# A peer step's second slab as moving operand of 512 columns, with results kept by tokens

## What is computed

```
def rmsnorm(x, g):                       # per token, over 1024 features
    y = x * rsqrt(mean(x * x) + 1e-6)
    return y * g
x = x + merged @ w_out                   # end of the first mixer
# peer_ffn(h): every token uses some of 16384 experts with weights gate
act = gelu(expert_u[idx] . h)
x = x + sum(gate * act * expert_v[idx])
x = rmsnorm(x, norm_final_g)             # end of the first block
# second block, layer 0
x = x + 0.5 * swiglu(rmsnorm(x, norm_ffn1), w_gate, w_up, w_down)
```

## Time and profile before

| | us |
|---|---|
| median of 3 runs | 2274.48 (2274.35 to 2275.05) |
| time of the profiled execution | 2271.26 |
| its span, first to last instruction | 2269.5 |
| TensorE busy in it | 2091.3 (92%) |
| VectorE busy | 1536.9 (68%) |
| ScalarE busy | 1036.3 (46%) |
| GpSimd busy | 67.7 (3%) |
| mean granted clock of TensorE | 0.97 |

### The profile page before, as it was taken

How to read it: one execution, slowest core, us unless ns; L and a number is a source line. 1 busy time by engine, 2 the same in 40 slices (tenths; PEclk the granted TensorE clock), 3 DMA queues, 4 the chain that set the end, 5 groups by cost and what they waited for, 6 DMA issues and landing times.

```text
span 2269.5 us, 45414 instructions
## 1 busy us (share of the span) xinstructions
PE 2091.3 (92%) x16952; PEld 2052.1 (90%) x16952; DVE 1536.9 (68%) x2526; ACT 1036.3 (46%) x1467; POOL 67.7 (3%) x41
## 2 busy tenths in 40 slices
PE   7898962789999999999999999979999999999997
PEld 7898862679999999999999999869999999889997
DVE  5677699976666666666667655676557555856555
ACT  4444320334444444444445554545445444555443
POOL 0000240000000000000000100000000000000000
PEclk9999985999999999999999999999999999999999
DMA  5334420015555555555554555425555555444553
GB/s 192 114 129 157 142 101 0 0 44 179 182 180 183 185 185 179 182 181 181 183 185 162 170 181 187 138 88 172 186 175 167 191 177 186 131 131 158 185 180 107
DMA packets 95684, 348.19 MB, mean 153 GB/s; under 512 B 10752, under 2 KB 10880, under 8 KB 95360
## 3 DMA queue, kind: packets, MB, share of 16 engines
q1 hardware_dynamic: 95184, 344.88, 46.2%
q10 hardware_dynamic: 432, 2.36, 0.3%
HBM read 346.15 MB, written 1.05 MB: 153 GB/s over the span
## 4 chain that ended last, share of the span: by engine, by line
PE 79%; DVE 14%; issue 3%; ACT 3%; DVEq 0%; DMA 0%; SPq 0%; ACTq 0%
PE front L1555 37%; PE acc L1555 29%; PE tile L1555 12%; DVE w_lo L901 2%; DVE pick L1333 2%; ACT w_hi L571 1%; DVE pick L1338 1%; DVE h_lo L933 1%; DVE rstd L925 1%; DVE onehot L1312 0%; DVE onehot L1316 0%; DVE idx L1320 0%; DVE top_i L1258 0%; DVE rest L1251 0%; DVE top_i L1247 0%
## 5 line engine op out<-in xcount | busy, mean ns | idle before, releaser
L901 DVE TENSOR_TENSOR w_lo<-raw,w_hi 128x1024 fp32r<-128x1024 f32 x636 | 783.5, 1232 | 204.1 <-ACT w_hi L571 203.6
L571 ACT CAST w_hi<-raw 128x1024 fp32r<-128x1024 f32 x652 | 679.5, 1043 | 372.4 <-PE front L1555 137.3
L1555 PE MATMUL front<-h_hi,w_hi 128*128 128x256 f32 x2432 | 690.2, 284 | 6.0 <-DVE h_lo L933 4.9
L1555 PE MATMUL front<-h_lo,w_hi 128*128 128x256 f32 x2432 | 688.2, 283 | 0.0
L1555 PE MATMUL front<-h_hi,w_lo 128*128 128x256 f32 x2432 | 688.1, 283 | 0.0
L1555 PE MATMUL acc<-mid_hi,w_hi 128*128 128x256 f32 x1728 | 491.4, 284 | 12.4 <-DVE mid_lo L1002 12.4
L1555 PE MATMUL acc<-mid_hi,w_lo 128*128 128x256 f32 x1728 | 490.4, 284 | 0.0
L1555 PE MATMUL acc<-mid_lo,w_hi 128*128 128x256 f32 x1728 | 490.3, 284 | 0.0
L1555 PEld LDWEIGHTS front<-h_hi,w_hi 128*128 128x128 f32 x2432 | 466.7, 192 | 8.0 <-DVE h_lo L933 5.6
L1555 PEld LDWEIGHTS front<-h_lo,w_hi 128*128 128x128 f32 x2432 | 466.8, 192 | 0.1
L1555 PEld LDWEIGHTS front<-h_hi,w_lo 128*128 128x128 f32 x2432 | 466.8, 192 | 0.0
(11 more groups left out here) (247 smaller groups left out, 1968.9 us busy)
## 6 DMA issues: line engine op xcount, KB each, us to landing
raw<-stream SPq DMA_DIRECT2D x652, 512.0 KB, 3.3
x<-x_t SPq DMA_DIRECT2D x2, 512.0 KB, 4.6
keysT<-keys_t ACTq DMA_DIRECT2D x1, 1024.0 KB, 6.5
attc<-attention_constants ACTq DMA_DIRECT2D x1, 1024.0 KB, 4.8
out_t<-h SPq DMA_DIRECT2D x4, 256.0 KB, 2.2
mixc<-mixer_constants SPq DMA_DIRECT2D x1, 704.0 KB, 9.0
wpool<-w_pool ACTq DMA_DIRECT2D x1, 256.0 KB, 5.1
lane<-lanes SPq DMA_DIRECT2D x1, 128.0 KB, 4.7
```

The source lines that it names most:

```text
L571: nc.scalar.copy(w_hi[:, s, :], raw[:, s, :]).then_inc(hi_ready, 1)
L901: nc.vector.tensor_tensor(w_lo[:, s, :], raw[:, s, :], w_hi[:, s, :].bitcast(F32), ALU.subtract).then_inc(lo_ready, 1)
L1555: return nc.tensor.matmul(out, lhsT, rhs, start=start, stop=stop, **kw)
```

## The change

In the peer steps the operands of `drain` change places. `mid` becomes stationary (128 experts x 128 tokens, one half of the tokens at a time) and the slab moves, 512 features at once: four banks (two token halves x two feature halves) with three matmuls each, 12 of 512 columns in the place of 24 of 256. `acc` then holds tokens on the partitions. The seeding follows: 16 matmuls of 128 columns with `x` as stationary operand in the place of 8 of 256.

At the end (`turn_x`) the sum of squares of a token is one row sum: ScalarE squares two banks with `accum_out`, takes the root of 128 x 1, VectorE inverts it and scales the banks into `x_tokens` (one quarter by ScalarE), TensorE turns 16 tiles of 128 x 128 back to features (identity kept in `eye`), and VectorE and ScalarE in turn, pair by pair, write `x` with the gain. `x` is then final, and the MLP behind starts with the ordinary norm. `weighted_norm`, `square_weights`, `gain_product`, `rstd_x`, the second root and GpSimd's four scalings of `x` are gone.

```diff
                     begin = s == 0 and not seeded and turn is None
-                    for m in range(KT):
+                    for b in range(4 if seeded else 0):
+
+                        a, c = [part[:, s % 2, b // 2 * P:(b // 2 + 1) * P] for part in (mid_hi, mid_lo)]
+                        hi, lo = [part[:, n % RING, b % 2 * D // 2:(b % 2 + 1) * D // 2] for part in (w_hi, w_lo)]
+                        mm(banks[:, b, :], a, hi, False, False, skip_group_check=True)
+                        mm(banks[:, b, :], c, hi, False, False, skip_group_check=True)
+                        ins = mm(banks[:, b, :], a, lo, False, False, skip_group_check=True)
+                        if last:
+                            ins.then_inc(bank_done, 1)
+                    for m in range(0 if seeded else KT):
...
+            def turn_x():
+
+                eps = cols[:, COL["eps"]:COL["eps"] + 1]
+                nc.scalar.activation(token_rms[:, 0:1], eps, ACT.Sqrt)
+                for tt in range(TT):
+                    act.wait_ge(bank_done, 2 * tt + 2)
+                    link(nc.scalar.activation(sq[:, 4 * tt:4 * tt + 4, :].rearrange("p a t -> p (a t)"),
+                                              banks[:, 2 * tt:2 * tt + 2, :].rearrange("p b n -> p (b n)"),
+                                              ACT.Square, accum_out=token_sums[:, tt:tt + 1]))
+                    nc.scalar.activation(token_rms[:, tt:tt + 1], token_sums[:, tt:tt + 1], ACT.Sqrt,
+                                         scale=1.0 / D, bias=eps).then_inc(token_roots, 1)
+                act.wait_ge(token_r_ready, TT)
+                nc.scalar.activation(x_tokens[:, 1, D // 2:], banks[:, 3, :], ACT.Copy,
+                                     scale=token_rms[:, 1:2]).then_inc(x_tokens_by_act, 1)
...
+                x_pair(1)
+                operand_hi(2, "norm_ffn1_0", [0, 1])
+                x_pair(3)
+                operand_hi(2, "norm_ffn1_0", range(2, KT))
...
-                if q == 3:
-                    weighted_norm()
-                elif q is not None:
+                if q is not None:
                     norm(q)
                 feed(1, n)
-                if q == 3:
-                    norm(3)
                 drain(0, n + fronts_)
```

More of the change, by code:

```diff
@@ L765, in _ @@
                 if kind == "ffn":
-                    mlp(ACT.Silu, first[f"ffn{i}"], FT, 2, done, (lambda: root(3)) if i == 0 else None)
+                    mlp(ACT.Silu, first[f"ffn{i}"], FT, 2, done)
                     done += FT
@@ L917, in inverse_rms @@
             def inverse_rms(q, late=None):
-                if q not in (0, 2, 3):
+                if q:
                     add_squares(q)
@@ L1356, in _, with token_rstd, scaled_tokens @@
                 mlp(first["peer"], NKEYS, 1, 0)
[L1358 to L1362, removed]
-                operand_lo(2, None, [6, 7])
+                def token_rstd(tt):
+                    dve.wait_ge(token_roots, tt + 1)
+                    nc.vector.reciprocal(token_rms[:, tt:tt + 1], token_rms[:, tt:tt + 1])\
+                        .then_inc(token_r_ready, 1)
+                    dve.wait_ge(token_r_ready, tt + 1)
+                def scaled_tokens(tt, half):
+                    nc.vector.tensor_scalar(x_tokens[:, tt, half * D // 2:(half + 1) * D // 2],
+                                            banks[:, 2 * tt + half, :], token_rms[:, tt:tt + 1], None,
+                                            ALU.mult).then_inc(x_tokens_by_dve, 1)
+                token_rstd(0)
+                scaled_tokens(0, 0)
+                scaled_tokens(0, 1)
+                token_rstd(1)
+                scaled_tokens(1, 0)
+                for pair in (0, 2):
+                    dve.wait_ge(x_turned, 2 * pair + 2)
+                    dve.wait_ge(x_ready, pair)
+                    for k in (2 * pair, 2 * pair + 1):
+                        ins = nc.vector.tensor_scalar(x[:, k, :], turned_x(k), col("norm_final_g", k), None, ALU.mult)
+                    ins.then_inc(x_ready, 1)
+                operand_lo(2, "norm_ffn1_0")
                 late = first["peer"] + 2 * NKEYS - 1 + RING
             done = NKEYS
-            q = 3
+            q = 2
             ys = 2
@@ L1789, in _ @@
                     wait_x(pe, 1, m)
-                    ins = mm(acc[:, m, :], ident, x[:, m, :], m % 2 == 0, False, skip_group_check=True)
+                    for tt in range(TT):
+                        ins = mm(banks[:, 2 * tt + m // 4, m % 4 * P:(m % 4 + 1) * P], x[:, m, tt * P:(tt + 1) * P],
+                                 ident, m % 4 == 0, False, skip_group_check=True)
                 ins.then_inc(x_seeded, 1)
@@ L1845, in _ @@
                 mlp(first["peer"], NKEYS, 1, 0, True, 0)
+                pe.wait_ge(eye_ready, 1)
+                for tt in range(TT):
+                    if tt == 0:
+                        pe.wait_ge(x_tokens_by_dve, 2)
+                    for k in range(KT):
+                        if tt and k == 0:
+                            pe.wait_ge(x_tokens_by_dve, 3)
+                        elif tt and k == KT // 2:
+                            pe.wait_ge(x_tokens_by_act, 1)
+                        ins = nc.tensor.transpose(turned_x(k)[:, tt * P:(tt + 1) * P],
+                                                  x_tokens[:, tt, k * P:(k + 1) * P], eye[:, :])
+                        if tt:
+                            ins.then_inc(x_turned, 1)
             done = NKEYS
-            q = 3
+            q = 2
             ys = 2
             for kind, i in layer_stages():
-                lows = 8 * (q - 1)
+                lows = 8 * q
                 q += 1
```

133 lines of the change are left out of this document (50 added, 83 removed).

## The result

The changed kernel takes 2250.53 us (median of 4 runs, 2249.44 to 2252.55), the kernel before 2274.41 (4 runs, 2272.38 to 2275.05). The ratio is 0.9899, with a 95% interval of 0.9884 to 0.9915: 23.9 us faster. I had forecast 2231.2 with a range of 2225 to 2249, so the time lies 1.5 us above the range; rival 1 had said 2248.5. The profiled execution took 2250.78 us, its span is 2248.9.

A forecast was written before the change was run, and what follows sets the result against it. The prediction took TensorE to bound the kernel; peer drains 37.8 us plus seam 5.5 made a gain of 43.3, so 2274.5 - 43.3 = 2231.2 us. The range was 2225 to 2249.

The forecast's parts named there:

- rival 1: Peer drains: 13.3 ns are added to each matmul, 512 columns take 226.7 ns, a step gains 0.16 us; 2248.5 us, 11%.
- What bounds the kernel, and what hides: Peer steps: TensorE alone bounds; VectorE goes from 67% to 71%, ScalarE from 47% to 50%, all stay hidden.
- again the floor of 120: Float32 records of 128 columns, one every 0.121 us, were read as showing the same 120 ns floor.
- my account: Peer drains: 120 ns is a floor hiding 256 columns' streaming; 512 columns take 213.3 to 218 ns; 82%.
- The nearest row: Peer drains: the float32 record of 256 columns, 0.2154 us, was taken as the price of a 512-column float32r matmul.
- The term for the peer drains: Peer drains: 12 matmuls at 0.2154 us for 24 at 0.120 gain 0.295 us a step, 37.8 us over 128 steps.
- rows 5 and 7: Earlier trace: half-clock matmul starts 213.8 ns apart; float32 records of 128, 256 and 512 columns at 0.121, 0.215, 0.430 us.
- The seam: Between peer steps and the MLP behind them: gain 7.0 us, less 1.5 for half clock, so 5.5, between 2 and 9.
- Seeding and start: Seeding 0.4 us more under a wait, identity copy and small gain products a few tenths each way; counted as nothing.
- Rivals 2 to 4: Peer drains, 512 columns: two of 256, 240 ns (3%, 2269 us); load alone, 120 (1%, 2085); half rate, 430 (3%, 2561).

The follow-up runs named there:

- the run with four widths: Changed kernel with the four banks of a peer drain moving 512, 384, 128 and 64 columns, three float32r matmuls each; 2146.83 us, one run.
- the kernel with the swap alone: Changed kernel, operands of the peer drains exchanged, but cut into 24 matmuls of 256 columns as before; 2262.22 us, ratio to before 0.9948.

## Why the prediction was wrong, point by point

**What bounds the kernel, and what hides.** Right. TensorE is at 500.00 of 500.00 us, VectorE at 68% where 71% was forecast, because the step came out longer, and feeds take 2.87.

**"A fixed cost that is added to each matmul would show there too. So at full clock the matmul waits for something that takes 120 ns whatever streams."** This is the step that failed. The added cost doesn't show at half clock, and still it is there at full clock: 384 columns take 174 to 175 ns and 512 take 226.6, 13 to 15 over the streaming time, and the floor for short matmuls in a row is 111. The load of the stationary operand, my likely owner, is not it: repeating its contents, changing the bank or halving its duration took at most 1.6 ns off, and a narrower one cost more.

**"again the floor of 120"** was a misreading, and the trace of the kernel before could have shown it. The 27 float32 records of 128 columns in the earlier trace rows cross a change of the clock: undisturbed starts are 111 or 112 ns apart up to 116.4 us and 213 or 214 from 116.8 us on, with some records missing or out of step, and 0.121 is no more than their average. The windows of the kernel before show the granted clock of the second part:

```profile
116.80:119.80 3.00, 3.00 (x24) 3.00 (x23) 2.93 (x6) 0.28 (x1) 0.00 (x0) 0.50 0.01 3
```

At full clock such a record takes 111 to 112 ns, less than 120 and the same as short float32r matmuls in a row take in the run with four widths. So the trace of before did show short matmuls that go faster than 120, and the 120 of 256 columns could not be a floor for all: the evidence for my account was one row weaker than I wrote, and rival 1 deserved more than 11%.

**The nearest row.** I took the float32 record of 256 columns, "the same 512 clocks of streaming behind the same load". It matched in clocks and not in what matters: it takes two clocks for a column, and such a matmul pays 2.5 ns. What the runs showed, for 256 to 512 columns:

| moving operand | spacing | clock | clocks a column | on top | load |
|---|---|---|---|---|---|
| float32r | 4 bytes | 2.4 GHz | 1 | 13.3 ns | 189 to 192 ns |
| bfloat16, every second | 4 bytes | 2.4 GHz | 1 | 11.7 ns | 96 to 97 |
| bfloat16, packed | 2 bytes | 2.4 GHz | 1 | 2.5 ns | 97 to 99 |
| float32 | 4 bytes | 2.4 GHz | 2 | 2.5 ns | 190 |
| float32r | 4 bytes | 1.2 GHz | 1 | 0 to 1 ns | not compared |

The cost is there where the moving operand advances by 4 bytes a partition in each clock of 2.4 GHz, and at most 2.5 ns where it advances half as fast. It does not follow the length of the load in the last column. That the pace of reading leaves no time in which the next stream's start could be hidden fits all five rows, but it is an argument; shown is only the dependence.

**The term for the peer drains** was 37.8 us and came as 128 x 0.14 = 17.9: 20 us, the whole miss. Rival 1 had its mechanism right and said 0.16 a step; the slow start takes 28 ns of it and the first short matmul behind gives 7 back. That its 2248.5 came as 2250.5 is in part luck: the profiled spans differ by 20.6 us where it had 26.0, and the 23.9 between the medians hold 3 us that the kernel before varies by. I gave it 11% because rows 5 and 7 spoke against it; the half-clock row and the long float32 ones spoke of matmuls that stream at half the pace, and the short float32 one was misread.

**The seam** was 5.5 (2 to 9) and came as 4.7. Nothing waits where I hadn't seen it; idle before the last drain is 0.81 us, and no half clock lies in it. The chain is longer by 0.4 until the turns (a root of one column takes 0.29 for 0.2, the scaled copies 1.41), and feed(0) takes 7.68 us for 48 matmuls that take 5.76 at full clock, partly at half clock (granted clock 0.58 over its first 4 us): the price I had put at 1.5 came as 1.9. By itself, with 256 columns, the seam gave 4.9.

**Seeding and start** at nothing: the start lost 1.1 us and the first peer drain 1.6, both by half-clock stretches that the kernel with the swap alone has too. I had not thought of a stretch that grows elsewhere.

**Rivals 2 to 4**: out. 226.6 to 236 ns, 228.9 on average, is not 240, not 120 and not 430; exchanging the operands is free.

## What to carry to other kernels

Before you price a change of a matmul's length, find out whether its time is a floor or a sum: one drain with 512, 384, 128 and 64 columns tells it. The nearest row must agree in how fast the moving operand advances, by element spacing and clocks a column, and not only in the clocks it streams; a half-clock stretch is no witness for full clock. And look at the distances inside a merged row, with the granted clock beside them, before you take its average for a price: here 0.121 was a mixture of 0.111 and 0.213. Where the precision of two bfloat16 parts is enough, packing them is worth far more in this kernel than longer matmuls: 143 us against 24.

## What the hardware showed beside that

- A change from 256 to 512 columns in float32r slows the first five long matmuls to 228 to 236 ns from 226.6, and the first short one behind long ones takes 113 ns for 120.
- 128 and 64 columns in float32r both take 111 ns with a load of 128 columns, except the first behind longer ones (60 ns) and the first of 64 behind those of 128 (79).
- The first bfloat16 matmul behind a float32r feed takes 11 to 13 ns more than the next ones (238.5 for 225, 226.6 for 215.8); behind a bfloat16 feed it doesn't (215.9).
- A stationary operand of 96 columns in float32r makes the load shorter and the matmul of 512 columns longer, 228 to 233 ns for 226.6. The run took 2254.48 us for the 2250.53 of the changed kernel, about what 128 drains of 28 ns more give (3.6 us).
- The kernel before and the one with the swap alone differ only in the seeding, the peer steps and the seam, and run the same late instructions at a different granted clock (0.96 and 1.00 between 1900 and 2060 us). That moved the profiled execution by 5.6 us in this stretch, more than the seam itself was worth.
